# A hybrid attention block on eight cores: transposes by DMA for the second norm and the heads' outputs, weight loads and multiplies placed anew

## What is computed

```python
xn = rmsnorm(x, norm_mix_g)
u = xn @ w_in                                   # conv gates, q, k, v, branch gates
g_a, g_b = split(sigmoid(u[..., g0:] + b_gate))
y_a = short_gated_conv(b_g, c_g, v_a, conv_w) @ w_a_out
o = diff_attention(q, k, v, lam, slopes)        # 4 heads, each two softmax maps of 64, values of 128
o = rmsnorm(o, subln_g) * (1.0 - lam_init)      # over each head's 128 columns
y_b = o.reshape(B, S, 512) @ w_b_out
x = x + (g_a * y_a + g_b * y_b) @ w_o
h = rmsnorm(x, norm_mlp_g) @ w_mlp_in           # "the second norm"
x = x + square(relu(h)) @ w_mlp_out
return rmsnorm(x, norm_final_g)
```

## Time and profile before

| | us |
|---|---|
| median of 3 runs | 1221.95 (1221.23 to 1222.13) |
| the profiled execution, its own time | 1218.94 |
| its span, slowest core (core 6) | 1217.4 |
| spans of the eight cores | 1213.7 to 1217.4 |
| granted TensorE clock, mean | 0.996 to 0.997 of 2.4 GHz |
| TensorE, VectorE, ScalarE, POOL busy | 95%, 49%, 54%, 7% |

### The profile page before, as it was taken

One profiled execution on the slowest core, in us unless ns is written; L12 is line 12 of the kernel. 1 busy time (PEld: TensorE's weight loads), 2 busy tenths in 40 slices (PEclk: granted clock), 3 DMA queues, 4 the chain that ended last, 5 costly groups with the idle time before them and its releaser, 6 DMA issues.

```text
span 1217.4 us, 27397 instructions; the slowest of 8 cores (1213.7 to 1217.4 us)
## 1 busy us (share of the span) xinstructions
PE 1154.6 (95%) x7340; PEld 578.0 (47%) x7464; DVE 601.8 (49%) x971; ACT 652.8 (54%) x1055; POOL 80.7 (7%) x139
## 2 busy tenths in 40 slices
PE   3799999999999999999999999999999999999995
PEld 1455444555555555554444444444444444444443
DVE  2666436553444333333365337336455463727767
ACT  4555358889898998976746773330211112030065
POOL 0000012111110000010000000000000000000012
PEclk9999999999999999999999999999999999999998
DMA  8487320002000000049441408011230403030124
GB/s 174 157 192 190 65 36 2 2 3 37 3 2 3 2 2 2 3 65 199 119 104 27 114 3 140 15 35 24 47 53 17 70 1 70 1 70 10 27 87 191
DMA packets 16903, 71.90 MB, mean 59 GB/s; under 512 B 2128, under 2 KB 2384, under 8 KB 14320
## 3 DMA queue, kind: packets, MB, share of 16 engines
q0 software_dynamic: 6768, 35.65, 17.9%
q1 hardware_dynamic: 9840, 33.97, 8.1%
q10 hardware_dynamic: 144, 0.52, 0.1%
HBM read 97.40 MB, written 8.39 MB: 87 GB/s over the span
## 4 chain that ended last, share of the span: by engine, by line
PE 88%; DMA 3%; DVE 3%; issue 3%; ACT 2%; DVEq 0%; SPq 0%; ACTq 0%; POOL 0%; POOLq 0%
PE ps_all L290 68%; PE ps_all L287 11%; PE ps_all L292 7%; DMA big<-w_g 2%; PE ps_all L311 2%; ACT big L582 1%; DVE big L314 1%; DMA big<-xs 1%; ACT big L298 0%; DVE big L1102 0%; DVE big L1120 0%; PE ps_all L657 0%; DVE big L625 0%; DVE big L974 0%; DVE big L1090 0%
## 5 line engine op out<-in xcount | busy, mean ns | idle before, releaser
L290 PE MATMUL ps_all<-big 128*128 128x512 bf16 (+2 forms) x4068 | 901.3, 375 | 27.2 <-DVE big L314 13.4
L290 PEld LDWEIGHTS ps_all<-big 128*128 128x128 bf16 x4192 | 394.3, 98 | 484.1 <-issue 43.1
L582 ACT ACTIVATE big<-ps_all,big 128x1024 bf16<-128x1024 f32 (+3 forms) x428 | 324.8, 802 | 38.2 <-PE ps_all L287 14.6
L1075 ACT ACTIVATE big<-ps_all 128x512 bf16<-128x512 f32 x124 | 74.1, 598 | 334.0 <-PE ps_all L290 333.8
L1102 DVE TENSOR_TENSOR big<-ps_all,big 128x512 f32<-128x512 f32 x256 | 176.6, 691 | 39.5 <-PE ps_all L290 36.1
L287 PE MATMUL ps_all<-big 128*128 128x129 bf16 x2176 | 163.6, 221 | 3.9 <-DVE big L625 1.8
L287 PEld LDWEIGHTS ps_all<-big 128*128 128x128 bf16 x2176 | 126.8, 98 | 54.5 <-issue 45.7
L1076 DVE TENSOR_TENSOR big<-big 128x512 bf16<-128x512 bf16 x124 | 53.0, 427 | 162.0 <-ACT big L1075 162.0
L292 PE MATMUL ps_all<-big 64*128 64x512 bf16 (+3 forms) x640 | 108.7, 352 | 3.6 <-ACT big L582 2.3
L298 ACT ACTIVATE big<-big 128x1024 bf16<-128x1024 f32 (+1 forms) x65 | 68.7, 1056 | 60.1 <-PE ps_all L290 25.2
L314 DVE TENSOR_TENSOR big<-ps_all,big 128x1024 bf16<-128x1024 bf16 (+1 forms) x49 | 58.9, 1205 | 40.7 <-PE ps_all L311 40.7
(11 more groups left out here) (60 smaller groups left out, 416.8 us busy)
## 6 DMA issues: line engine op xcount, KB each, us to landing
big<-xs SPq DMA_DIRECT2D x48, 512.0 KB, 6.5
big<-w POOLq DMA_DIRECT2D x16, 1024.0 KB, 12.8
big<-w_g POOLq DMA_DIRECT2D x16, 512.0 KB, 7.9
out<-big SPq DMA_DIRECT2D x15, 512.0 KB, 2.6
big<-w_in POOLq DMA_DIRECT2D x12, 512.0 KB, 8.0
big<-w_o POOLq DMA_DIRECT2D x1, 2048.0 KB, 24.4
big<-w_a POOLq DMA_DIRECT2D x1, 1024.0 KB, 10.9
big<-w_b POOLq DMA_DIRECT2D x1, 1024.0 KB, 11.0
```

The costliest lines, as they stand in the source:

```text
L290: S.op("pe", lambda e: e.matmul(out, lhsT, rhs, start=start, stop=stop), reads=reads, writes=writes)
L582: S.op("act", lambda e, a=a, b=b, bi=bi: e.activation(PT[:, :, a:b], Sps[:, buf, :, a:b], AF.Exp, bias=btab[:, bi:bi + 1], scale=0.125), r ...
L1075: S.op("act", lambda e: e.activation(r, ph, AF.Relu), reads=[phk], writes=[rk])
```

## The change

- The second norm's transposes leave TensorE: `turn_rows` issues one DMA transpose of 128x1024 bf16 for each tile on SP's queue, in the step of the scaling, from `xb2_ring` into `xn2T_all`. The norm's vector is multiplied in place in `xn2T_all` by VectorE (`mul2`), three steps after the issue, which is two steps later than the multiply stood.
- The heads' transposes leave TensorE: one DMA transpose of 128x512 for each head, issued by SP right behind the head's normalisation. The head norm's vector is now a row `gsr`, loaded to all partitions and scaled once on POOL ahead of attention, and multiplied in the normalisation: four scalar_tensor_tensor of 128 columns in place of one tensor_tensor of 512. The eviction from bank 7, `emit_flip`, `rest_flips` and the planner's rules for them go.
- ScalarE writes the squares of the second norm's statistics, which nobody reads, to PSUM banks 6 and 7 and not to `xb`.
- W1(0) alone is put on the queue after step 23. W2(0) and W1(1) come after the fourth and the eighth MLP group and wait for a square of the third and the seventh; `gfin` comes after the twelfth.

In the diff, lines are left out that only declare or drop names.

```diff
@@ -293,9 +293,10 @@
                  reads=reads, writes=writes)
 
     def row_stats(x, xkey, ntok, xb, xbkey):
+        xb = xb[:ntok]
         st, skey = stats[:ntok, stat_n[0]:stat_n[0] + 1], "stat%d" % stat_n[0]
         stat_n[0] += 1
-        S.op("act", lambda e: e.activation(xb[:ntok], x[:ntok], AF.Square, accum_out=st),
+        S.op("act", lambda e: e.activation(xb, x[:ntok], AF.Square, accum_out=st),
              reads=[xkey, "stat0s"], writes=[xbkey, skey])
         S.op("act", lambda e: e.activation(st, st, AF.Ln, bias=epsc[:ntok, 0:1], scale=1.0 / D_MODEL),
              reads=[skey, "epsc"], writes=[skey])
...
@@ -314,6 +315,9 @@
         S.op("dve", lambda e: e.tensor_tensor(dst, pst[:, :, :ntok],
                                               gcols.unsqueeze(2).to_broadcast([128, 8, ntok]), ALU.mult),
              reads=[pkey, gkey], writes=dkeys)
+
+    def turn_rows(xb, xbkey, dst, dkeys):
+        S.dma("sp", lambda e: e.dma_start_transpose(dst, xb), reads=[xbkey], writes=dkeys)
 
     evac_flip = [0]
 
...
@@ -502,17 +504,20 @@
     assert hb_off <= C_OFF + 8192 and ar.p >= C_OFF + 16384
     at["on"] = [ar.take([128, 4, 128], BF16) for _ in range(2)]
     WA_OFF = TOT - 8192
+    gsr = ar.take([128, 128], F32)
     assert ar.p <= WA_OFF
     Wa = region(WA_OFF, 8192).take([128, 4, 1024], BF16)
-    at_keys = ["att0", "att1", "att2", "ato", "aton0", "aton1", "atrec", "atss", "atrs"] + hb_ring.keys + cg_ring.keys + acc_ring.keys
+    at_keys = ["att0", "att1", "att2", "ato", "aton0", "aton1", "atrec", "atss", "atrs", "gsr"] + hb_ring.keys + cg_ring.keys + acc_ring.keys
     S.reuse(at_keys + ["Wa"], up_keys)
     S.reuse(["ya%d" % i for i in range(4)], xn_keys(4) + xn_keys(5))
     wload(Wa, w_a, "Wa")
+    ld("sp", gsr, gsub_d.partition_broadcast(128), "gsr")
+    S.op("pool", lambda e: e.tensor_scalar(gsr, gsr, (1.0 - LAM_INIT) * math.sqrt(128.0), None, ALU.mult),
+         reads=["gsr"], writes=["gsr"])
 
     Sps = ps_all[:, 0:2048].rearrange("p (b m n) -> p b m n", b=2, m=2)
     Ops = ps_all[:, 2048:3584].rearrange("p (b n) -> p b n", b=3)[:, :, 0:387].rearrange("p b (g v) -> p b g v", g=3)
     OB_KEYS = ["pb4", "pb5", "pb6"]
-    Tps = bank(7).bitcast(BF16)[:, 0:512].rearrange("p (q t) -> p q t", q=4)
     S.op("dve", lambda e: e.memset(Ops[:, 2, 2, :], 1.0), writes=["pb6"])
 
     steps = []
...
@@ -644,22 +648,14 @@
         yield rs
 
         def fin_():
-            flip_at[n] = LAT + dve(lambda e: e.tensor_tensor(
-                on, o, ss[:, 4:8].unsqueeze(2).to_broadcast([128, 4, 128]), ALU.mult),
-                ["ato", "atrs"], [onk], 0.69, clk["pool"] + LAT)
+            for q in range(4):
+                dve(lambda e, q=q: e.scalar_tensor_tensor(on[:, q, :], o[:, q, :], ss[:, 4 + q:5 + q], gsr,
+                                                          ALU.mult, ALU.mult),
+                    ["ato", "atrs", "gsr"], [onk], 0.22, clk["pool"] + LAT)
+            i, h = steps[n]["i"], steps[n]["h"]
+            turn_rows(on.rearrange("p q v -> p (q v)"), onk,
+                      O_n[:, h, i * 512:(i + 1) * 512].rearrange("p (q t) -> p q t", q=4), ["qo%d_%d" % (i, h)])
         yield (fin_, "pool")
-
-    def emit_flip(n):
-        st = steps[n]
-        i, h = st["i"], st["h"]
-        on, onk = at["on"][st["hid"] % 2], "aton%d" % (st["hid"] % 2)
-        for qc in range(4):
-            S.op("pe", lambda e, qc=qc: e.transpose(Tps[:, qc, :], on[:, qc, :], ident),
-                 reads=[onk, "ident"], writes=["pb7"])
-        clk["pe"] += 0.35
-        b7["free"] = LAT + dve(lambda e: e.tensor_scalar_mul(
-            O_n[:, h, i * 512:(i + 1) * 512].rearrange("p (q t) -> p q t", q=4), Tps, gsub[:, 1:2]),
-            ["pb7", "gsub"], ["qo%d_%d" % (i, h)], 0.48, clk["pe"] + LAT)
 
     b7 = dict(free=0.0)
     q_ready = {0: 0.0}
...
@@ -843,12 +838,6 @@
         frac = min(1.0, cum[qk_n] / SPAN)
         if not side["end"]:
             r_side = b7["free"] if side["whole"] else 0.0
-        if flips and side["whole"] and flip_at.get(flips[0], BIG) <= t and b7["free"] <= t:
-            set_mode(0)
-            emit_flip(flips.pop(0))
-            continue
-        if flips and flip_at.get(flips[0], BIG) <= t and side["whole"]:
-            r_side = BIG
         ahead = side["done"] - N_SIDE * frac
         if r_qk <= t:
             pick = "qk"
...
@@ -907,7 +895,8 @@
     x_mid = region(KT_OFF, 65536).take([128, 16, 1024], F32)
     kv_keys = ["KT%d_%d" % (h, b) for h in range(4) for b in range(8)] + ["V%d" % k for k in range(32)] + ["Vones"]
     S.reuse(["xm%d" % T for T in range(16)], kv_keys)
-    pst_ring = Ring([bank_bf_T(6), bank_bf_T(7)], "pst", keys=["pb6", "pb7"])
+    junk = bank(6, 2)
+    S.reuse(["pb6"], ["pb7"])
     mm_ring = Ring([bank(b) for b in range(0, 4)], "pmm", keys=["pb%d" % b for b in range(0, 4)])
     z_ring = Ring([bank(b) for b in (4, 5)], "pz", keys=["pb4", "pb5"])
     load_gate_w(0, 1)
...
@@ -1011,24 +993,28 @@
         x = x_mid[:, T, :]
         if name == "act2":
             xb, xbkey = xb2_ring.next()
-            st2[T] = (xb, xbkey) + row_stats(x, "xm%d" % T, 128, xb, xbkey)
+            st2[T] = (xb, xbkey) + row_stats(x, "xm%d" % T, 128, junk, "pb6")
         elif name == "dve2":
             xb, xbkey, st, skey = st2[T]
             row_scale(x, "xm%d" % T, 128, xb, xbkey, st, skey)
-        else:
+        elif name == "post2":
             xb, xbkey, st, skey = st2[T]
-            flip_rows(xb, xbkey, 128, gmlp, "cst", xn2T_all[:, :, T * 128:(T + 1) * 128],
-                      ["xn2T_%d" % T, "ya%d" % i] + ["qo%d_%d" % (i, h) for h in range(4)], pst_ring)
+            xT = xn2T_all[:, :, T * 128:(T + 1) * 128]
+            turn_rows(xb, xbkey, xT, ["xn2T_%d" % T, "ya%d" % i] + ["qo%d_%d" % (i, h) for h in range(4)])
+        if name == "mul2":
+            xT = xn2T_all[:, :, T * 128:(T + 1) * 128]
+            S.op("dve", lambda e: e.tensor_tensor(xT, xT, gmlp.unsqueeze(2).to_broadcast([128, 8, 128]), ALU.mult),
+                 reads=["xn2T_%d" % T, "cst"], writes=["xn2T_%d" % T])
 
     ev2 = {}
     for i in range(4):
         for t in range(4):
             base = 16 * (i // 2) + 8 + 4 * (i % 2) + t
-            for name, off in (("act2", 0), ("dve2", 1), ("post2", 2)):
+            for name, off in (("act2", 0), ("dve2", 1), ("post2", 1), ("mul2", 4)):
                 ev2.setdefault(base + off, []).append((name, i, t))
 
     def run_ev2(j):
-        for nm in ("post2", "dve2", "act2"):
+        for nm in ("mul2", "dve2", "post2", "act2"):
             for (name, i, t) in ev2.get(j, []):
                 if name == nm:
                     do_ev2(name, i, t)
...
@@ -1126,7 +1112,7 @@
     for j, fn in enumerate(flat):
         fn()
         run_ev2(j)
-        if j == 27:
+        if j == 23:
             S.reuse(["W1_0"], ["Wa"])
             S.reuse(["W1_1"], ["Wb"])
             S.reuse(["W2_0"], ["Wg2", "Wg3"])
...
@@ -1134,16 +1120,22 @@
             S.reuse(r_ring.keys + xbf_ring.keys, tf_ring.keys)
             S.reuse(h2_keys, [k_ for i in range(4) for k_ in xn_keys(i)])
             load_w1(0)
-            load_w2(0)
-            load_w1(1)
     S.reuse(["gfin"], ["Wo"])
-    ld("sp", gfin, gfin_d.partition_broadcast(128), "gfin")
     j = len(flat)
     for sl in range(4):
         for fc in range(4):
             mlp_in(0, sl, fc)
+            if fc == 3 and sl in (0, 1):
+                key = "h2_0_2_%d" % sl
+                wk = ("W2_0", "W1_1")[sl]
+                S.reuse([wk], [key])
+                (load_w2, load_w1)[sl](sl)
+            if fc == 3 and sl == 2:
+                S.reuse(["gfin"], ["h2_0_2_2"])
+                ld("sp", gfin, gfin_d.partition_broadcast(128), "gfin")
             run_ev2(j)
             j += 1
+    S.reuse(["pb7"], ["pb6"])
     for g in range(1, 7):
         if g >= 2:
             load_w1(g)
```

## The result

The changed kernel takes 1228.8 us (median of 6 runs) against 1222.0 us for the kernel before on the same chip: ratio 1.0051, 95% interval 1.0036 to 1.0066. It is slower by 0.5%. Two of the six runs are slow ones, in which the cores of one die show a lower clock; the ratio is that of the other four, whose median is 1227.8 us. I had forecast 1210.0 us, with 0.14 for slower. The profiled execution took 1229.61 us around a span of 1228.0 us (core 2). The cores lie between 1218.0 and 1228.0 us, their granted clock between 0.985 and 0.990 (0.996 to 0.997 before).

What follows compares the result with a forecast made beforehand. TensorE, busy 1154.6 of 1217.4 us, was taken as the bound. Terms -7.2 - 1.6 - 3.5 + 0.3 = -12.0 us, off the median of 1221.95, gave 1210.0 us; forecast range 1205 to 1213 (chance 0.62), wider range 1205 to 1217 (0.8).

Steps and rivals of the forecast that it cites:

- no limit there: Heads' DMA transposes in attention: no reader before their columns' gate step, buffers reused after two heads, so landing time sets no limit.
- How long a transpose takes: Landing time of a DMA transpose, the unknown of the case: taken as 3 to 5 us, from a store's 2.6 us.
- packet bound: Upper limit on a norm transpose's landing: 1024 row packets over 16 engines at 0.16 us each, 10.3 us.
- The limit of 6.2 us: Output projection: the scaling of tile T+2 waits for T's transpose, leaving 6.2 us to landing before VectorE waits.
- The norm's transposes, -7.2: Output projection: eight TensorE transposes removed from each of 16 tiles, 0.45 us a tile, saving 7.2 us.
- The MLP's start, -1.6: First MLP groups: TensorE's idle times of 0.56 and 1.05 us before the last two tiles' transposes go, saving 1.6 us.
- The heads' transposes, -3.5: Attention, one head in the first gate step: TensorE loses 16 x 0.23 us; taken as -3.5, bounded by 0 and -7.
- even sixteen times 1.9 fit into the rest: nothing: Attention: up to 1.9 us more VectorE work a head costs nothing, as VectorE is busy 155 of 365 us.
- Rival C: Attention gives nothing, as ScalarE and the planner's new order take it back, and POOL's wait costs 2.8: 1216, chance 0.10.
- The moved loads, 0 to +2: MLP weight loads issued later, around the second projection and MLP start, still arrive about in time: 0, at most +2 us.
- The row's load and its POOL multiply, 0 to +2.8: Attention's start: gsr's load and POOL multiply ahead of the first affine_select cost 0, or +2.8 us at the far end.

Runs made afterwards that it cites:

- e1: Changed kernel without the wait of merged[1]'s first writes for the readers of aton0, aton1 and gsr: 1211.5 us, ratio 0.9915.
- e3: Changed kernel with the heads' part undone: TensorE's transposes kept for the heads, everything else of the change taken: 1210.7 us, ratio 0.9915.
- e12: e11 made complete: the head norm's vector and its constant multiplied once into the rows of w_b: 1220.4 us on an uneven chip, ratio 0.9907.
- e14: Kernel of e12 and e13, with W2(0) also waiting for the second norm's last two DMA transposes: 1218.0 us on the uneven chip, ratio 0.988.
- e4: Kernel before with the heads' part of the change alone; second norm and MLP loads as before: 1238.0 us, ratio 1.0135.
- e9: Kernel before with each head's four TensorE transposes done twice: 1224.3 us, ratio 1.0023.
- e10: e8 without the heads' DMA transposes, so the heads' outputs are not transposed at all: 1209.3 us, ratio 0.9904.
- e11: e5 with one tensor_tensor of 512 columns per head for the four scalar_tensor_tensor, the head norm's vector left out: 1202.4 us, ratio 0.9844.
- e5: e1 with gsr scaled on VectorE just before the first head's normalisation, not on POOL: 1208.4 us, ratio 0.990.
- e2: Changed kernel, wait kept, with the loads of w_g(0,1) and w_o held until the last head's transpose has landed: 1215.2 us, ratio 0.9954.
- e8: e5 with TensorE's old order and one tensor_tensor of 512 columns per head, the head norm's vector left out: 1213.0 us, ratio 0.9942.
- e13: The same kernel as e12, run again on an even chip: 1213.2 us, ratio 0.9927.

## Why the prediction was wrong

**The step that failed** is "The heads' transposes have no reader until the gate step of their columns, and their buffers come round after two heads: no limit there". I asked who reads the result and when the ring comes round. I did not ask which later writers the kernel makes wait for the readers of the source buffers. The transpose is a reader of `aton0` and `aton1`. On core 2 of before TensorE's transposes of the last head are done at 538.0, 1.9 us behind the normalisation; the DMA transpose has landed 31 us behind it (542.84 to 574.12). The first writer of `merged[1]` waits for it, by a list that names more buffers than lie there. That is +17.1 us in a forecast of -12.0. Without it (e1) the kernel takes 1211.5 us, 1.5 over my number, though by errors that cancel: attention gives nothing of its -3.3, and the last stage gives 5.3 in place of 2.5.

**How long a transpose takes** was not the error I feared. I took 3 to 5 us; in after the norm's land in 2.8 us and the heads' in 2.4 (medians; 4.3 and 4.4 at most, but for the last head's). My packet bound had the count right (1056 packets for each of the norm's, (26,736 - 9840) / 16 by SP's queue in e3) and the price wrong: with an engine to itself a packet of 256 bytes costs no more than 2.8 x 16 / 1056 = 0.04 us, not 0.16. What I lacked was the neighbour: I gave the weight loads a price when they stand next to each other, none when they stand next to a transpose. This came in twice, at the 16th head and at W2(0).

**The limit of 6.2 us** for the scaling of tile T+2 was the right one, but up to 3.7 us go by from VectorE's end to the record of the issue on SP, which I had left out. VectorE in the first projection of after, one tile and the next two:

```profile
644.16 0.74 DVE L307 TENSOR_SCALAR big<-big 128x1024 bf16<-128x1024 f32 x1
...
647.00 0.69 DVE L984 TENSOR_TENSOR big<-ps_all,big 128x512 f32<-128x512 f32 x1 [0.97 <-PE ps_all L290]
647.61 0.74 DVE L307 TENSOR_SCALAR big<-big 128x1024 bf16<-128x1024 f32 x1
...
650.45 0.69 DVE L984 TENSOR_TENSOR big<-ps_all,big 128x512 f32<-128x512 f32 x1 [0.96 <-PE ps_all L290]
651.53 0.75 DVE L307 TENSOR_SCALAR big<-big 128x1024 bf16<-128x1024 f32 x1 [0.39 <-DMA big<-big]
```

The scaling ends at 644.90, the issue's record starts at 648.59, the landing is some 2.8 us later, at 651.4: 6.5 us in all. The wait of 0.39 us for it is there, once, at the third scaling. For this first tile the margin I thought to be 1 to 3 us is gone; the issues of the next two come 3.2 and 2.0 us behind their scaling.

**The norm's transposes, -7.2:** right. The adds of first halves lie 3.45 us apart (647.00, 650.45), as forecast. Of the 16 tiles 14 lie between the two marks: 14 x 0.45 = 6.3, less 0.3 for VectorE, gives 136.2; measured 136.5 in after, 136.5 to 136.9 in the runs that have this part, but for the uneven chip of e12 and e14.

**VectorE in the projection, +0.3:** right. The multiply in place takes 1218 ns, against 1.28 for the nearest row. **ScalarE's square into PSUM, 0:** right, 1028 ns and no wait.

**The MLP's start, -1.6, and the last two tiles, -0.9:** the waits are gone, but the stage lost 5.3 us, not 2.5. In e4, where the norm's part is unchanged, it is already 2.1 us shorter (455.7). The trace of before shows a candidate. VectorE, then POOL (start, us), near the end:

```profile
1191.86 2.26 DVE L1090 TENSOR_TENSOR big<-big 128x256 bf16<-128x256 bf16 x1
...
1195.51 0.28 DVE L1090 TENSOR_TENSOR big<-big 128x256 bf16<-128x256 bf16 x1
```

```profile
1191.62 2.35 POOL L1117 TENSOR_TENSOR big<-big 128x1024 f32<-128x1024 f32 x1 [2.84 <-ACT big L1115]
```

The square that starts while POOL multiplies two operands from SBUF ends just after POOL does, at 1194.12 against 1193.97; its like takes 0.28. In e4 the same square runs at 1213.02 and POOL's multiply starts at 1213.13: it slips through. No run was made of this alone; it is a reading of two traces. The other 0.7 us are not accounted for.

**The heads' transposes, -3.5:** too high as a price, and wrong as a result. In the old order doubling them costs 2.8 us (e9), and taking them and their evictions away gives 1.0 (e10 against e3; 1.6 on the four cores of e10 without a clock drop); the 5.1 us of e11 come mostly from the new order. The step that failed is "even sixteen times 1.9 fit into the rest: nothing" for VectorE. Its time rose by 1.72 - 0.70 - 0.48 = 0.5 us a head, well inside my bounds, and VectorE is idle more than half of the stage. But the copy-out of the next head's sums waits behind the four instructions on the same queue, and value matmuls wait for it; behind the longest of these waits TensorE's granted clock falls to half, which my sum had at 1.00 throughout. Together that is the 5.4 us between e5 and e11. Free time on an engine says nothing of an instruction that stands in front of one that TensorE waits for. Rival C had attention at zero for another reason, ScalarE and the order; the order was a gain.

**The moved loads, 0 to +2:** right in after. Not in e1, e2, e8, e12 and e13, where the last stage lost up to 11.6 us on a core: I had asked when W2(0) and W1(1) are needed, not which transfer is in flight when they are issued. **The row's load and its POOL multiply, 0 to +2.8:** the load lands in 5.7 us, TensorE waits 1.7 us on the profiled core, which takes 366.7 us for attention; the median of the cores loses nothing that can be measured (e5).

**What stays open:** in e13 on core 5 only 144 packets of W2(0), nine an engine, go by during the 18.0 us of the transpose, and W2(0) itself takes 17.5 us; one for one gives some 10 us of this, and why both then drag on at a DMA share near 0.1 is not known. Nor is it shown by a run of its own that the clock drops of attention come from the waits ahead of them.

## What to carry over

When a reader of a buffer moves from an engine to a DMA, look up every wait that names this buffer, and whether it has to: a list that names too much cost nothing while the reader was quick. Take for the landing the time beside the transfers that are queued there, not the time alone. A DMA transpose is many small packets: keep it and large loads from the software queue apart, by a wait on the load if need be. An engine that is half idle still makes others wait; before one instruction is cut in four, see what stands behind it. A wait of TensorE can cost more than its length, by the clock that it brings down.

## What the runs showed of the hardware

- A DMA transpose from SBUF to SBUF lands 2.4 us (128x512 bf16) and 2.7 to 3.1 us (128x1024) after its issue in most cases, with 1.2 us for the issue on SP; between the producer's end and that issue lie 0.9 us for the first head of after, core 2, and 3.7 us for the 16th. Queued with weight loads the last head's took 25.2 to 29.0 us in after, and one of 128x1024 up to 18.0 us in e13.
- It is 544 or 1056 packets. Beside the weight loads the two queues were served nearly packet for packet: 510 of 256 bytes and 527 of the loads in 21.7 us.
- TensorE's granted clock fell to 0.50 in a stall of 15.3 us and stayed there for 11 matmuls after it (4.34 us).
- It also fell to that level behind waits of 1.34 and 1.79 us in attention (e5, core 0), for some 3.5 us each time, and stayed at 1.00 where these waits were 0.20 and 0.78 us (e11). One such drop cost 1.3 us.
- A VectorE multiply of two SBUF operands, 0.28 us by itself, took 2.26 us beside a POOL multiply that had started 0.24 us earlier. The Trainium skill, "SBUF — State Buffer", section "Who interferes with whom", says that the two contend and that the later one stands still until the other is done. The end times agree.
